# Turning the normed input in two halves around the first products of each stage, with products of constants before them

## The reference

```
first stack, per layer:
    h = rms_norm(x, pre_mix_norm);   mix = attention_mixers(h @ w_in) @ w_o
    x = x + rms_norm(mix, post_mix_norm)
    h = rms_norm(x, pre_ffn_norm);   f = (silu(h @ gate) * (h @ up)) @ w_down
    x = x + rms_norm(f, post_ffn_norm)
second stack, per layer (nsa, stick-breaking, convolution, moba):
    h = rms_norm(x, attn_norm);      x = x + mixer(h @ w_in) @ w_out
    h = rms_norm(x, mlp_norm);       x = x + square(relu(h @ w_up)) @ w_down
```

## Time and profile before

| | |
|---|---|
| time, median of 3 runs (lowest to highest) | 1972.51 us (1969.75 to 1977.07) |
| time of the profiled execution | 1971.99 us |
| span of its records | 1970.2 us |
| mean granted TensorE clock | 0.973 |
| PE busy | 1862.5 us, 95% |
| DVE, ACT, POOL busy | 1136.8, 922.4, 167.3 us (58%, 47%, 8%) |

### The profile page before, as it was taken

One profiled execution on the slowest core, in us unless ns is written; L12 is line 12 of the kernel. 1 busy time (PEld: TensorE's weight loads), 2 busy tenths in 40 slices (PEclk: granted clock), 3 DMA queues, 4 the chain that ended last, 5 costly groups with the idle time before them and its releaser, 6 DMA issues. The chain is left out here.

```text
span 1970.2 us, 28964 instructions
## 1 busy us (share of the span) xinstructions
PE 1862.5 (95%) x11496; PEld 1630.1 (83%) x11496; DVE 1136.8 (58%) x1647; ACT 922.4 (47%) x1267; POOL 167.3 (8%) x213
## 2 busy tenths in 40 slices
PE   7899999889899989899999999999889999989998
PEld 6668999766899978689998789998669998769997
DVE  6576555757555578564545465446755446765443
ACT  4564334456434446554435364345235434564432
POOL 1300000040000020001000001002400102000000
PEclk9999999999999999799999999999989999989999
DMA  7504555640355555125555425554724454525551
GB/s 246 181 22 140 179 183 184 184 167 20 120 192 192 189 186 174 53 94 206 175 205 175 171 86 173 202 179 171 212 91 169 174 191 165 187 96 173 176 206 67
DMA packets 185356, 313.07 MB, mean 159 GB/s; under 512 B 18878, under 2 KB 67572, under 8 KB 185268
## 3 DMA queue, kind: packets, MB, share of 16 engines
q1 hardware_dynamic: 182595, 304.24, 45.7%
q0 software_dynamic: 1376, 4.38, 0.8%
q10 hardware_dynamic: 1296, 3.24, 0.5%
HBM read 309.90 MB, written 1.94 MB: 158 GB/s over the span
## 5 line engine op out<-in xcount | busy, mean ns | idle before, releaser
L1451 DVE TENSOR_TENSOR w_lo<-raw,w_hi 128x2048 fp32r<-128x2048 f32 (+2 forms) x290 | 652.1, 2279 | 297.7 <-ACT w_hi L987 296.9
L987 ACT ACTIVATE w_hi<-raw 128x2048 fp32r<-128x2048 f32 (+2 forms) x290 | 533.3, 1876 | 108.1 <-PE tr L1989 59.8
L1987 PE MATMUL acc<-w_hi,hT_hi 128*128 128x512 f32 (+2 forms) x688 | 268.7, 391 | 10.9 <-DVE w_lo L1451 6.8
L1989 PE MATMUL acc<-w_hi,hT_lo 128*128 128x512 f32 (+2 forms) x688 | 266.3, 387 | 0.0
L1988 PE MATMUL acc<-w_lo,hT_hi 128*128 128x512 f32 (+2 forms) x688 | 266.0, 387 | 0.0
L1987 PE MATMUL acc<-w_hi,aux_hi 128*128 128x512 f32 x608 | 237.1, 390 | 0.0
L1988 PE MATMUL acc<-w_lo,aux_hi 128*128 128x512 f32 x608 | 237.1, 390 | 0.0
L1989 PE MATMUL acc<-w_hi,aux_lo 128*128 128x512 f32 x608 | 236.5, 389 | 0.0
L1987 PE MATMUL up<-hT_hi,w_hi 128*128 128x256 f32 x768 | 217.7, 283 | 0.6 <-DVE w_lo L1451 0.6
L1987 PE MATMUL tr<-hT_hi,w_hi 128*128 128x256 f32 x768 | 217.3, 283 | 0.0
L1988 PE MATMUL tr<-hT_lo,w_hi 128*128 128x256 f32 x768 | 217.3, 283 | 0.0
(11 more groups left out here) (357 smaller groups left out, 2748.5 us busy)
## 6 DMA issues: line engine op xcount, KB each, us to landing
raw<-in_mlp_w_up SPq DMA_DIRECT2D x64, 1024.0 KB, 6.7
raw<-in_mlp_w_down SPq DMA_DIRECT2D x64, 1024.0 KB, 5.4
raw<-in_ffn_w_gate_up SPq DMA_DIRECT2D x88, 512.0 KB, 4.8
raw<-in_ffn_w_down SPq DMA_DIRECT2D x22, 1024.0 KB, 5.0
raw<-in_w_in SPq DMA_DIRECT2D x16, 1024.0 KB, 8.0
raw<-in_sb_w_in SPq DMA_DIRECT2D x12, 1024.0 KB, 5.7
raw<-in_moba_w_in SPq DMA_DIRECT2D x12, 1024.0 KB, 5.3
raw<-in_nsa_w_in SPq DMA_DIRECT2D x10, 1024.0 KB, 5.4
```

Source lines behind the costliest of these rows:

```text
L987: nc.scalar.activation(w_hi[:, p0.slot, 0:p0.floats], raw[:, p0.slot, 0:p0.floats], ACT.Copy)\
L1451: nc.vector.tensor_tensor(w_lo[:, p0.slot, 0:m], raw[:, p0.slot, 0:m], f32(w_hi[:, p0.slot, 0:m]), ALU.subtract).then_inc(sem["lo_ready"], 1)
L1987: nc.tensor.matmul(dst, hi, whi, start=first, stop=False)
L1989: return nc.tensor.matmul(dst, lo, whi, start=False, stop=last)
```

## The change

The turning of x is cut in two batches of eight transposes, `tr` (channels 0 to 511) and `up` (512 to 1023).

- At an **x junction** the first batch (`first_half`) stands within the stage before, ahead of its last 12 products (the second piece, t = 1, of the last chunk or of the last `down`). DVE makes those four pieces of `hT_lo` (`turned_lo`) before it adds x's second half. The second batch (`second_half`) stands behind the next stage's first 12 products (`gemm`) or first 24 (`ffn`), and waits there for x's second half.
- At a **y junction** the first batch stays in `norm`. Ahead of it PE issues nine products of constants (`keep_clock`: a matrix of ones with 128 x 256 of the constants, into a bank that nobody reads). DVE makes the first four pieces of `hT_lo` before it writes x's second half (`y_added(1)`). The second batch stands where it does at an x junction.
- In `ffn` variant A's last `down`, tile 1's products of the first column half now come before those of the second, with a signal between, and ACT squares the first half's sum on that signal.
- The kernel's first norm keeps its order.

```diff
+    for a, b in zip(phases, phases[1:]):
+        if b.kind == "norm":
+            a.then, b.before = b, ("y" if a.out == "y" or a.variant == "A" else "x")
+        if a.kind == "norm":
+            b.opens = a
...
# ACT, ffn variant A
                     for t in range(TT):
-                        if t == 0:
-                            act.wait_ge(sem["tile_done"], n["tile_done"] + 1)
-                        else:
-                            act.wait_ge(sem["piece_used"], end)
                         for b in range(2):
+                            if (t, b) == (1, 1):
+                                act.wait_ge(sem["piece_used"], end)
+                            else:
+                                act.wait_ge(sem["tile_done"], n["tile_done"] + t + 1)
                             y_square(acc[:, 2 * t + b, :], t, b)
...
# DVE
+            def norm(ph):
+                if ph.before != "x":
+                    turned_lo(ph, range(KT // 2))
+                if ph.before == "y":
+                    y_added(1)
+                turned_lo(ph, range(KT // 2, KT))
                 dve.wait_ge(sem["ss_ready"], n["ss_ready"] + TT)
                 root(norm_rstd, ss[:, 0:TT], D).then_inc(sem["rstd_ready"], 1)
...
+                    if ph.out == "x" and i == 1:
+                        turned_lo(ph.then, range(KT // 2))
                     dve.wait_ge(sem["piece_used"], pieces[-1][0] + 1)
...
# PE
+            def norm(ph):
+
+                if ph.before == "x":
+                    return
+
+                if ph.before is None:
+                    pe.wait_ge(sem["x_landed"], 16)
+                    pe.wait_ge(sem["vec_evac"], 1)
+                    turn_x((0, 1, 2, 3))
+                    return
+                if ph.layer is None:
+                    keep_clock(acc[:, 3, 0:S], 9)
+                else:
+                    keep_clock(up[:, 1, 0:S], 9)
+                pe.wait_ge(sem["x_written"], n["x_written"] - 2)
+                turn_x((0, 1))
+
+            def keep_clock(bank, count):
+
+                for _ in range(count):
+                    nc.tensor.matmul(bank, cb("ones"), both[:, 0:S], start=True, stop=True)
+
+            def second_half():
+
+                pe.wait_ge(sem["x_written"], n["x_written"])
+                turn_x((2, 3))
+
+            def first_half():
+
+                pe.wait_ge(sem["x_written"], n["x_written"] + 2)
+                turn_x((0, 1))
...
# PE, gemm
+                            if ph.opens is not None and ph.opens.before is not None and (i, k0, t) == (0, 0, 0):
+                                second_half()
+                            if ph.out == "x" and (i, k0, t) == (1, PK, 0):
+                                first_half()
...
# PE, ffn: hidden, then down
+                            if steps[0] == 0 and (j, a) == (0, 1):
+                                second_half()
...
+                            if ph.variant == "A" and final and t == 1:
+                                for b in (0, 1):
+                                    for k in range(ph.kt):
...
+                                    if b == 0:
+                                        last.then_inc(sem["tile_done"], 1)
+                                continue
...
+                            if ph.then is not None and ph.variant == "B" and final and (j, t) == (1, 0):
+                                first_half()
```

More of the change, by code:

```diff
@@ L174, in __init__ @@
         self.mix = None
+        self.then = None
+        self.opens = None
+        self.before = None
         self.row, self.l, self.uq, self.ukv, self.cmp = row, l, uq, ukv, cmp
@@ L1000, in norm @@
                     g = gain_col[:, ph.gain + k:ph.gain + k + 1]
-                    nc.scalar.activation(hT_hi[:, k, :], norm_bank(ph, k // 2)[:, S * (k % 2):S * (k % 2) + S], ACT.Copy,
+                    nc.scalar.activation(hT_hi[:, k, :], norm_bank(k // 2)[:, S * (k % 2):S * (k % 2) + S], ACT.Copy,
                                          scale=g).then_inc(sem["hT_hi"], 1)
@@ L1477, in root, with turned_lo @@
                 return nc.vector.scalar_tensor_tensor(out=dst, in0=t, scalar=1.5, in1=dst, op0=ALU.add, op1=ALU.mult)
-            def norm(ph):
-                for k in range(KT):
+            def turned_lo(ph, ks):
+                for k in ks:
                     dve.wait_ge(sem["hT_hi"], n["hT_hi"] + 2 * (k // 2) + 2)
@@ L1528, in add_y, with y_added @@
             def add_y(last_gain):
-                sums, r = ss[:, 6:8], rstd[:, 0:TT]
+                sums = ss[:, 6:8]
                 halves = ss[:, 2:6].rearrange("p (t b) -> p t b", b=2)
                 link(nc.vector.tensor_tensor(sums, halves[:, :, 0], halves[:, :, 1], ALU.add))
[L1533 to L1538, removed]
-                        nc.vector.scalar_tensor_tensor(out=x[:, t, c], in0=h[:, t, c], scalar=r[:, t:t + 1],
-                                                       in1=x[:, t, c], op0=ALU.mult, op1=ALU.add)\
-                            .then_inc(sem["x_written"], 1)
+                link(root(rstd[:, 0:TT], sums, D))
+                y_added(0)
+                last_gain()
+            def y_added(b):
+                for t in range(TT):
+                    c = slice(W * b, W * b + W)
+                    nc.vector.scalar_tensor_tensor(out=x[:, t, c], in0=h[:, t, c], scalar=rstd[:, t:t + 1],
+                                                   in1=x[:, t, c], op0=ALU.mult, op1=ALU.add)\
+                        .then_inc(sem["x_written"], 1)
             def unit_pipeline(us, extra={}):
@@ L1960, in ffn @@
                     for b in range(2):
+                        if b == 1 and ph.then is not None:
+                            turned_lo(ph.then, range(KT // 2))
                         dve.wait_ge(sem["piece_used"], end - 1 + b)
@@ L1989, in three, with turn_x @@
                 return nc.tensor.matmul(dst, lo, whi, start=False, stop=last)
-            def norm(ph):
-                for j in range(KT // 2):
-                    if n["x_written"]:
-                        pe.wait_ge(sem["x_written"], n["x_written"] - 4 + (2 if j < 2 else 4))
-                    else:
-                        pe.wait_ge(sem["x_landed"], 16)
-                        pe.wait_ge(sem["vec_evac"], 1)
+            def turn_x(js):
+                for j in js:
                     for k in range(2):
@@ L2001, in norm @@
                             c = P * (2 * j + k)
-                            last = nc.tensor.transpose(norm_bank(ph, j)[:, S * k + P * t:S * k + P * t + P], x[:, t, c:c + P],
+                            last = nc.tensor.transpose(norm_bank(j)[:, S * k + P * t:S * k + P * t + P], x[:, t, c:c + P],
                                                        ident)
                     last.then_inc(sem["hT_tr"], 1)
+            def norm(ph):
[21 more added lines that the diff above has]
+                turn_x((0, 1))
             def gemm(ph):
```

9 lines of the change are left out of this document (6 added, 3 removed).

## The result

| | before | changed |
|---|---|---|
| time, median (lowest to highest) | 1973.90 us (1969.75 to 1977.36, 13 runs) | 1958.35 us (1954.89 to 1967.30, 13 runs) |
| profiled execution | 1971.99 us | 1959.28 us |
| its span; mean granted clock | 1970.2 us; 0.973 | 1957.5 us; 0.981 |

The ratio of the changed kernel to the one before is 0.9933, with a 95% interval of 0.9920 to 0.9946: 0.7% faster, 10.7 to 15.8 us. Ten more runs, taken beside later experiments, gave a median of 1962.34 us and a ratio of 0.9943 (0.9926 to 0.9959).

The account below looks back on a forecast made before the run. PE, busy 95% of the span, was taken to bound the kernel; 7.6 us at y junctions plus 3.7 us at x junctions made 11.3 us off the profiled 1971.99, so 1960.7 us, range 1955 to 1969.5.

Parts of the forecast that it names:

- Constants cost nothing, and keep the clock: y junctions: nine products on PE take 4.2 us, end 0.2 us before x's first half, cost nothing, change the clock.
- First product at T + 6.4: First y junction: next stage's first product 6.4 us behind T, the last product's end, where before it came at T + 8.09.
- The 0.2 us for low pieces: y junctions: first 12 products use a piece every 0.36 us, DVE makes one every 0.41: 0.2 us more.
- The second junction's waits: Second y junction: PE waits 0.4 us for x's second half and 1.0 us for the weight split; gain 0.9 us.
- The 0.4 us of waiting for x's second half: Second y junction: first chunk's 12 products of 416 columns end at T + 8.7, then PE waits 0.4 us.
- x junctions, 3.7 us: Seven x junctions: 3.9 us of waits for x's second half go, less 0.2 us for entries: gain 3.7 us.
- the term of 0.2 for entries: x junctions: two entries into products after transposes now, 0.03 us taken per junction, 0.2 us off the gain.
- I take nothing: Later squares, root and splits still fit, so no cost taken; upper bound 1 us at each of 11 junctions.
- The room of 0.5 us for the splits: Stick-breaking layer's x junction: split done at T' + 11.3, PE wants it at T' + 11.8; T' ends the old stage's products.
- The rivals: Clock falls at y junctions: 1969 us, chance 0.13; splits late in part: 1967, 0.12; splits late in full: 1983, 0.05.
- The splits came late: Rival, chance 0.12: PE waits up to 1 us for `w_lo` at each junction, 1964 to 1972 us, taken as 1967.
- the first rival: y junctions: clock falls all the same between constants and first real product, 1.2 to 3.1 us each; 1969 us, chance 0.13.

Follow-up runs that it names:

- x junctions alone: x junctions as in the changed kernel, y junctions' order, constants and early square as in the kernel before; median 1966.61 us, ratio 0.9961.

## Why the prediction was right, and where it was not

The forecast was 1960.7 us, or 11.3 off the profiled execution; the changed kernel's two medians are 1958.35 and 1962.34, and its profiled execution 12.7 us shorter.

- **Constants cost nothing, and keep the clock.** Right. Nine take 4.05 us and end 0.38 before x is there; 18 show what they cost beyond the wait. Without them the gain is gone (34.9 us lost instead of 25.3).
- **First product at T + 6.4.** It came at T + 6.7 at all four: the way from the transposes over ACT and DVE was mis-sized by 0.3 us. So the y junctions gave 1.4, 0.7, 2.1 and 1.9 us, 6.1 instead of 7.6. The 0.2 us for low pieces that come slower than the first 12 products use them did not show: these products run at the full pace from the start.
- **The second junction's waits.** Right in kind. The prediction's terms for the split add up to T + 17.56, where it writes 17.7, against T + 16.81: 0.75 us of waiting, for which it takes 1.0. Measured were 0.69. The 0.4 us of waiting for x's second half did not come; the second batch starts at T + 9.1 straight behind the products.
- **x junctions, 3.7 us.** The sum came out because two errors cancelled, which is luck. The first is the size of the waits. The printed idle time starts at the end of the last transpose's record; by the distance between starts, the 0.63 us of the earlier trace rows are 1056.89 - 1055.23 - 0.87 = 0.79 (its row is `1056.89 1.09 PE L2002 MATMUL up<-both,x 128*128 128x128 f32 x8 [0.63 <-DVE x L1965]`). So the seven junctions lost some 5.5 us, not 3.9, and what stood around a wait went with it, which the term of 0.2 for entries had the wrong way. The second is "I take nothing" for late squares: it followed the splits on ACT and DVE and left out POOL, which waits for the same squares, and PE waited 1.1 us for POOL. The room of 0.5 us for the splits held at six junctions, and was short by 0.31 at the one before the moba layer, which lost 0.7 with what stands around the wait.
- **The rivals.** The clock did not fall in the 2.6 us between constants and first product, and filling them changed nothing. The splits came late at two places, by 1.0 us together.
- **What I had not weighed** is that at y junctions the constants alone would do it. I counted the order and the clock in one sum; the old order with the full clock loses 5.8, the new one 6.1. Nor had I weighed that the loss of before, 31.4 us, is that of one execution: the same order shows 27.3 in another kernel's profile, so the 6.1 us of gain hang in part on the profile that they are counted from.
- 6.1 and 3.7 make 9.8 of the profile's 12.7 us. The rest lies in the stretches outside the junctions, where the lower clock took 3.5 us less (some 1.5 us of time at 0.44) and 1.4 us stay open. The prediction had 1.5 too much at the y junctions and nothing of these 2.9 us; that its total is off by only 1.4 is luck too.

As the prediction read the rule of the Trainium skill that transposes don't count as busy time ("TensorE: Matmul & The Clock Gate", "Part 4: PE-mode transpose"), the constants would not help past their own end, and the first rival follows. That did not come: the clock held over a batch with idleness on both sides of it, 2.6 us with products of constants right before and real products right behind. The fall of the earlier trace rows does not decide it, since it also stands behind 4.28 us of idleness. The run with the x junctions alone speaks against the rule: near the end of PE's wait or just behind it the clock fell, and it was back at the full level by the second product at all four y junctions, at the fourth within the second batch, when PE had done nothing since the wait but transposes. At the third junction of the kernel before, 16 transposes did not bring it back before the first products. So transposes can bring the clock back; when they do stays open.

## What to carry to other kernels

Where TensorE waits for a chain that can't be shortened, products of constants as long as the wait, and no longer, keep the clock up for the work behind it; price them from a row, and look what the chain's length leaves. Test the clock and the order apart: here a reordering that starts work earlier was worth nothing at the full clock, and without the constants it was the slower one, by 4.8 us in the medians. Look at the granted clock in every profile before you count in it, also at places that the edit leaves as they are. When an instruction moves later, follow every engine that waits for it or for what is queued behind it, the one that is 9% busy too.

## What the runs showed of the hardware

- A float32 product of 128 x 128 by 256 columns stands in the trace as two records, 0.216 us apart (36 records in 7.77 us with 18 constants), so 0.43 us at the full clock; the rounded form takes 0.12. A float32 transpose of 128 x 128 takes 0.11.
- Nine such products in a wait of 4.4 us kept the granted clock at 1.00 at four places where it was 0.65 to 0.75 without them.
- After a wait of 4.3 to 5.0 us the clock came back to the full level with only float32 transposes, 16 at most, and at most one product behind the wait (x junctions alone, all four y junctions; 3.4 us at the lower level at each).
- The same program's executions differ by up to 14 us, nearly all of it through the clock: time at the lower level costs 0.42 to 0.44 us per us, and leaves 0.9 us of scatter. A change of 2 us is visible in rows long before it is in medians.
